# Weight splits placed behind the treatment of a result and bounded to four tiles ahead; the first input laid out by features

## The reference, cut to what matters

```
qkv = x @ w_qkv;  q, k, v = split(qkv, 3)
q = apply_rope(q) * 64 ** -0.5;  k = apply_rope(k)
for each block of 128 queries, each head, both maps m:
    p[m] = softmax(where(allowed, q[m] @ k[m].T, min))
    a = p[0] - lam * p[1];  o = a @ v
o = rms_norm(o) * (1 - lambda_init);  mix = o @ w_o
x = layer_norm(alpha * x + mix)
x = layer_norm(alpha * x + (silu(gate) * up) @ w_out)      # gate, up = split(x @ w_in, 2)
```

## Time and profile before

| | |
|---|---|
| timed runs | 1912.24 us median (1912.19 to 1922.69) |
| the profiled execution's own time | 1916.28 us |
| its span, first to last instruction | 1914.6 us |
| PE busy | 1841.1 us, 96% of the span |
| DVE, ACT, POOL busy | 903.6, 664.8, 57.9 us |
| mean granted TensorE clock | 0.984 of full speed |
| hi: 236 + 53 instructions, mean | 1059 and 1057 ns |
| lo: 236 + 53 instructions, mean | 1225 ns |

### The profile page before, as it was taken

One profiled execution on the slowest core, in us unless ns is written; L12 is line 12 of the kernel. 1 busy time (PEld: TensorE's weight loads), 2 busy tenths in 40 slices (PEclk: granted clock), 3 DMA queues, 4 the chain that ended last, 5 costly groups with the idle time before them and its releaser, 6 DMA issues.

```text
span 1914.6 us, 21555 instructions
## 1 busy us (share of the span) xinstructions
PE 1841.1 (96%) x8656; PEld 1480.3 (77%) x8656; DVE 903.6 (47%) x1544; ACT 664.8 (35%) x1084; POOL 57.9 (3%) x68
## 2 busy tenths in 40 slices
PE   8987879999999999999999999999999999999998
PEld 6755557888888897566698888888887788888886
DVE  3576766533333362555573333336544474334343
ACT  4233432422223232555432232222446444323231
POOL 0221110000000000000000000000000000000000
PEclk9989899999999999999999999999999999999999
DMA  7321111423333323222223333333321324333221
GB/s 235 98 77 49 66 53 56 132 77 112 98 99 99 120 87 107 66 67 67 83 89 99 93 95 99 99 98 96 100 73 60 110 67 122 99 100 99 77 78 44
DMA packets 217306, 174.51 MB, mean 91 GB/s; under 512 B 8899, under 2 KB 177765, under 8 KB 217206
## 3 DMA queue, kind: packets, MB, share of 16 engines
q1 hardware_dynamic: 217206, 173.13, 29.7%
HBM read 170.97 MB, written 7.38 MB: 93 GB/s over the span
## 4 chain that ended last, share of the span: by engine, by line
PE 90%; DVE 5%; ACT 3%; issue 2%; DMA 0%; SPq 0%; ACTq 0%
PE ps L526 27%; PE ps L527 27%; PE ps L528 27%; PE ps L823 2%; PE ps L783 2%; ACT whi L989 1%; PE ps L803 1%; PE ps L833 1%; PE ps L845 1%; PE ps L722 1%; DVE wlo L1263 1%; PE ps L793 0%; PE ps L934 0%; DVE arena L1289 0%; DVE arena L1285 0%
## 5 line engine op out<-in xcount | busy, mean ns | idle before, releaser
L1263 DVE TENSOR_TENSOR wlo<-raw,whi 128x1024 fp32r<-128x1024 f32 x236 | 288.3, 1225 | 588.8 <-ACT whi L989 586.6
L989 ACT ACTIVATE whi<-raw 128x1024 fp32r<-128x1024 f32 x236 | 248.8, 1059 | 578.3 <-PE ps L528 570.8
L526 PE MATMUL ps<-xh,whi 128*128 128x512 f32 (+1 forms) x1176 | 444.9, 378 | 0.0
L528 PE MATMUL ps<-xh,wlo 128*128 128x512 f32 (+1 forms) x1176 | 433.2, 368 | 0.0
L527 PE MATMUL ps<-xl,whi 128*128 128x512 f32 (+1 forms) x1176 | 433.1, 368 | 0.0
L526 PE MATMUL ps<-whi,hh 128*128 128x512 f32 x648 | 257.1, 397 | 7.2 <-DVE hl L1467 3.8
L526 PEld LDWEIGHTS ps<-xh,whi 128*128 128x128 f32 x1176 | 224.0, 190 | 39.0 <-issue 4.6
L528 PE MATMUL ps<-whi,hl 128*128 128x512 f32 x648 | 253.8, 392 | 0.0
L527 PE MATMUL ps<-wlo,hh 128*128 128x512 f32 x648 | 253.6, 391 | 0.0
L528 PEld LDWEIGHTS ps<-xh,wlo 128*128 128x128 f32 x1176 | 223.2, 190 | 37.4
L527 PEld LDWEIGHTS ps<-xl,whi 128*128 128x128 f32 x1176 | 223.6, 190 | 36.7 <-issue 2.9
(11 more groups left out here) (198 smaller groups left out, 2021.7 us busy)
## 6 DMA issues: line engine op xcount, KB each, us to landing
raw<-in_ffn_w_in SPq DMA_DIRECT2D x88, 512.0 KB, 3.9
raw<-in_w_ff SPq DMA_DIRECT2D x64, 512.0 KB, 4.0
raw<-in_ffn_w_out SPq DMA_DIRECT2D x44, 512.0 KB, 3.8
raw<-in_a_w_qkv SPq DMA_DIRECT2D x24, 512.0 KB, 5.2
raw<-in_w_in SPq DMA_DIRECT2D x20, 512.0 KB, 3.8
raw<-in_kv_w SPq DMA_DIRECT2D x16, 512.0 KB, 3.7
bias_skewed<-bias_rows SPq DMA_DIRECT2D x8, 640.0 KB
raw<-in_a_w_o SPq DMA_DIRECT2D x8, 512.0 KB, 4.7
```

The lines of the kernel that those rows point to most:

```text
L526: e.matmul(o, ah, bh, start=start, stop=False)
L528: return e.matmul(o, al, bh, start=False, stop=stop)
L989: e.activation(self.parts(m)[0], self.raw[:, m % RAW, :], ACT.Copy).then_inc(s.hi, 1)
L1263: e.tensor_tensor(lo, self.raw[:, m % RAW, :], f32(hi), ALU.subtract).then_inc(s.lo, 1)
```

## The change

A constant `AHEAD = 4` replaces the bound of eight. `pump` is no longer called by `done`; it is called by `take` as before, and once, for at most one split, at the end of `post`, behind the post step. The host hands the kernel a second copy of x, laid out by features; SP loads it in four pieces of 512 KB, each ahead of the weight tile that is used with it, and the transpositions and the split of their banks are gone for this first input. The x by positions, which the first residual needs, is loaded in the step `prepare_a`. The loads of norm vectors and tables come behind the first half of the value rows, and those rows now go one tile at a time. Of the two `xt` steps below, the first is ACT's and the second DVE's; the loop over `RAW` is SP's.

```
-        while most and self.slots and not self.waiting and self.n_split < len(self.tiles) + SPLIT + EXTRA:
+        while most and self.slots and not self.waiting and self.n_split < len(self.tiles) + AHEAD:
...
     def done(self, tile, sem, value):
...
-        self.pump()
...
     def post(self, job):
...
             self.step("post", job, None)
+        self.pump(1)
...
     def network(self):
         self.step("table", LN_EXP)
-        for t in range(4):
-            self.feat(0, t)
-            self.xsplit(0, t)
+        values = self.rows("v", ("a_w_qkv", 2048), 0, 8, hh=False)
+        for i in range(16):
+            if i % 4 == 0:
+                self.step("xt", i // 4)
+            next(values)
         self.step("load_norm", 1)
         self.step("load_a")
-        self.run(self.rows("v", ("a_w_qkv", 2048), 0, 8, grouped=True, hh=False))
+        self.run(values)
...
-                    w.wait_ge(s.xl, x_at + 2 * t + 2)
+                    w.wait_ge(s.xl, x_at + (8 if x_at else k0 + 2))
...
+            elif what == "xt":
+                j, = arg
+                w.wait_ge(s.xt[j], 16)
+                e.activation(self.xh[:, 2 * j:2 * j + 2, :], self.xt[:, 2 * j:2 * j + 2, :],
+                             ACT.Copy).then_inc(s.xh, 2)
...
+            elif what == "xt":
+                j, = arg
+                c = (slice(None), slice(2 * j, 2 * j + 2), slice(None))
+                w.wait_ge(s.xh, 2 * j + 2)
+                e.tensor_tensor(self.xl[c], self.xt[c], f32(self.xh[c]), ALU.subtract).then_inc(s.xl, 2)
...
                 if r.kind == "res":
                     w.wait_ge(s.rows, r.value)
+                    w.wait_ge(s.x[t], 16)
...
+        for m in range(RAW):
+            c = (slice(None), slice(2 * m, 2 * m + 2), slice(None))
+            e.dma_start(self.xt[c], ap["c_xt"][c]).then_inc(s.xt[m], 16)
+            weights(m)
         e.dma_start(self.ident[:], ap["c_ident"]).then_inc(s.ident, 16)
-        for t in range(4):
-            e.dma_start(self.x[:, t, :], ap["x"][0, t * 128:t * 128 + 128, :]).then_inc(s.x[t], 16)
-        for m in range(RAW):
-            weights(m)
...
             elif what == "prepare_a":
+                for t in range(4):
+                    e.dma_start(self.x[:, t, :], ap["x"][0, t * 128:t * 128 + 128, :]).then_inc(s.x[t], 16)
...
+def features_first(x):
+
+    return np.ascontiguousarray(x[0].reshape(S, 8, 128).transpose(2, 1, 0))
```

More of the change, by code:

```diff
@@ L24 @@
 EXTRA = 2
+AHEAD = 4
 FFN_GROUPS = [(0, 6), (6, 8), (14, 8)]
@@ L199, in projections, with rows @@
             self.run(self.quarters(*w))
-    def rows(self, kind, source, row0, nk, k_first=0, grouped=False, hh=True, norm=None, group=0):
+    def rows(self, kind, source, row0, nk, k_first=0, hh=True, norm=None, group=0):
         blocks = [(k_first + k) % nk for k in range(0, nk, 2)]
@@ L213, in rows @@
                 runs = [[k] for k in blocks[:-n]] + [blocks[-n:]]
-            elif grouped:
-                runs = [blocks[:n]] + [[k] for k in blocks[n:]]
             else:
@@ L535, in __init__ @@
         self.raw = [new(f"raw{i}") for i in range(RAW)]
-        self.x = [new(f"x{i}") for i in range(4)]
+        self.x, self.xt = [new(f"x{i}") for i in range(4)], [new(f"xt{i}") for i in range(4)]
         self.g = [new(f"g{i}") for i in range(3)]
@@ L631, in __init__ @@
         self.qk_a.append([ar(BASE + 13824 + i * 512, 512) for i in range(3)])
+        self.xt = ar(BASE + 8192, 4096).rearrange("p (k c) -> p k c", k=8)
         self.V = ar(BASE + 4096, 4096).rearrange("p (t c) -> p t c", t=4)
@@ L713, in tensor @@
                     w.wait_ge(*freed[b])
-                    if norm == 0:
-                        w.wait_ge(s.x[t], 16)
-                    elif norm < 4:
+                    if norm < 4:
                         w.wait_ge(s.ln, 8 * (norm - 1) + 2 * t + half + 1)
@@ L993, in scalar @@
                 for half, b in enumerate(banks):
-                    w.wait_ge(s.feat, 8 * norm + 2 * t + half + 1)
+                    w.wait_ge(s.feat, 8 * (norm - 1) + 2 * t + half + 1)
                     e.activation(self.xh[:, half * 4:half * 4 + 4, t * 128:t * 128 + 128],
@@ L1104, in scalar @@
                 if t >= 2:
-                    w.wait_ge(s.feat, 8 * norm + 2 * (t - 2) + 2)
+                    w.wait_ge(s.feat, 8 * (norm - 1) + 2 * (t - 2) + 2)
                 elif norm == 5:
-                    w.wait_ge(s.feat, 8 * 4 + 2 * (t + 2) + 2)
+                    w.wait_ge(s.feat, 8 * 3 + 2 * (t + 2) + 2)
                 e.activation(self.y[t % 2], self.x[:, t, :], ACT.Square,
@@ L1815 @@
     given["a_w_qkv"] = halves_first(given["a_w_qkv"])
+    given["c_xt"] = features_first(given["x"])
     given.update(constants())
```

## The result

The kernel after takes 1863.74 us (median of four runs, 1862.75 to 1865.22), the kernel before, run beside it, 1914.38 us. The ratio is 0.9728, 95% interval 0.9697 to 0.9760: faster by 2.7%. The profiled execution took 1865.22 us, with a span of 1863.5 us and a mean granted clock of 0.995, where the one before had 0.984. Its span is 51.1 us shorter.

A forecast was written before the change was run, and what follows sets the result against it. PE was taken to bound the full networks, with waits and lowered clock in the first attention. Gains of 29 there, 5.5 at the start and 1 in the second attention, 35.5 us, gave 1880.8, or 1877 us as median; range 1854 to 1902.

The forecast's parts named there:

- Ten waits by 2.32 us, 23 in all: First attention: PE's ten waits on the treatment (line 1289) each fall by hi and lo's 2.32 us, at most 23 us.
- 5 us given back, 2 us gained on line 1459: First attention: lo delaying softmax work costs 5 us (0 to 8.6); two softmax-result waits shorten by 2 us.
- The clock, 9 us: First attention: waits fall by 44%, so 44% of the 21 us lost by clock, 9 us, comes back.
- the clock coming back entirely: First attention, rival: remaining short waits no longer lower the clock, 12 us more return, 1865 us; chance 0.13.
- The start, 5.5 us: Kernel start: without the transpositions PE starts at 8.9 instead of 14.26 us; 5.5 us less, between 1.5 and 8.
- The second attention, 1 us (0 to 4): Second attention: the post step's ACT copy gets out from behind hi; 1 us less, between 0 and 4.
- SP, POOL and the networks, nothing: Moved loads on SP and POOL's queued addition are covered, and full PE hides the move in the networks; no change.
- POOL's port, nothing: DVE's lo beside POOL's work: no charge, since lo kept its duration beside a mask; blocking rival 1888 us, chance 0.05.
- DVE as the bound: First attention, rival: DVE becomes the bound because lo is only moved; 17 us gained with the start, 1896 us; chance 0.17.

The follow-up runs named there:

- experiment 4: Kernel after with the old bound of eight, so each split follows directly behind the treatment of the job that frees its slot; 1867.61 us, ratio 0.9723.
- experiment 5: Kernel after with each split one step earlier, ahead of the treatment, in a slot freed a job earlier; 1886.79 us, ratio 0.9832.
- experiment 11: Kernel after plus 40 small matmuls before the first product, just-treated bank passed over once, bound of eight in the first attention; 1866.15 us, ratio 0.9725.
- experiment 12: Kernel after plus 25 small matmuls before the first product, just-treated bank passed over once, bound of eight in the first attention; 1863.01 us, ratio 0.9726.
- experiment 1: Kernel after with splits placed as before (bound of eight, pump in `done`, none in `post`), only the start differing from the kernel before; 1926.13 us, ratio 1.0038.
- experiment 9: Kernel after with the bound of four only until the first half of the value rows, then bound of eight and pump in `done`; ratio 0.9986.

## Why the prediction was right, step by step

Direction, size and mechanism were right: 1877 us forecast, 1863.74 measured, inside 1854 to 1902. The terms against the traces, for 35.5 us forecast and 51.1 us of span found (the execution forecast from, at 1916.28 us, lay 4.0 us above the median then known; the profiled execution of the kernel after lies 1.5 above its own):

- **Ten waits by 2.32 us, 23 in all.** Measured 32.6 - 10.3 = 22.3. Experiments 4 and 5 show that the place of lo behind the treatment makes them, as the step had it. Its other half, that hi no longer waits for a running job, is true in the trace (ACT's waits for PE ahead of hi fall from 19.5 us in 12 to 2.8 in one) but adds nothing here once lo stands behind (experiment 4).
- **5 us given back, 2 us gained on line 1459.** The line costs 5.4 us in two waits before and 5.9 in seven after, so both came and all but cancelled. The two waits of 2.83 and 2.58 us are 1.26 and 1.30 now, 2.9 us less; five new ones of 0.4 to 1.0 us make 3.4. With each lo directly behind its treatment it is 6.3. PE's idle time fell by 23.1 us, not by 20: these two terms were 2.5 us too gloomy, the first 0.7 too hopeful, and a wait for ACT fell by 1.3.
- **The clock, 9 us.** In the first attention this is the step that was mis-sized most: 13 us came back by PE's busy time, 15 by the clock column. The proportion to the waiting time was the error. In the kernel before, each of the 12 spells of low clock in the stage starts within 1.3 us of the end of a wait of 1.9 us or more. Of such waits it has 14, and the kernel after four, with three spells: their number falls faster than the sum of the waits (45.5 to 22.4 us). Nine spells at 1.6 us (experiments 11 and 12) are 14 us. So of the named rivals, the clock coming back entirely (1865) lay nearest to the result. That its time fits is luck in part: 6 us of the 21 are still lost, and the second attention brought 5.5 us that it did not have. The Trainium skill, "TensorE: Matmul & The Clock Gate", section "HAM oscillation — how this bites in real kernels", has the cost of a fallen clock paid anew behind each wait for the next slice, so that it goes with the number of such waits. The traces agree that it goes by spells (1.6 us each); that of two equal waits (2.04 and 2.03 us) one has a spell and the other none, they show beyond it.
- **The start, 5.5 us.** Measured 6.0. PE started at 8.38 (8.9 forecast) and the fourth pair was not late. The first 13 products at 0.43 us cost 2.6 us, as the prediction let stand. But the term was reckoned as if it stood by itself; experiments 1 and 9 show that it needs the bound at the start, and that without it the first scores come 6.8 us later than before.
- **The second attention, 1 us (0 to 4).** Measured 6.5, outside the bounds given. The split out of ACT's way was the right place: the wait on line 1490 went from 4.9 to 0.5 us, and 3.2 us of the gain go where the bound of eight is back (experiment 4). One spell of low clock at its start went too. That PE loses only 7.7 us there bounded the idle time, not what could come back with the clock; and most of those 7.7 us were waits for the very copy that the step moved.
- **SP, POOL and the networks, nothing.** Right: 363.87 against 363.88 us in the network, and no wait up to 79 us in spite of the loads that moved.
- **POOL's port, nothing.** Nearly right in size, wrong in its reason. The earlier trace rows showed lo beside a mask. Behind the treatment lo meets POOL's rotary addition instead, and there the trace shows blocking (last section). POOL has time for its own part; but four times the longer addition holds up an operation of the softmax on DVE (line 1468) by 0.9 us, and PE's waits on line 1472 behind these four are 1.30, 0.43, 0.13 us and none, so an estimate is that at most 0.9 + 0.43 + 0.13 = 1.5 us are lost.
- **DVE as the bound.** It did not come: no wait of PE on DVE in the stage is longer than before, though DVE is busy for 159.98 of 197.15 us, 81%. (The prediction's 79% is 163 of 208 us, 78%.)
- **Not foreseen:** 1.6 us lost in the mixer, to one more spell of low clock while PE was full, and 3.6 gained in its last part, where a wait of 1.85 us became 0.28 and the spell behind it went. Why the clock falls with no wait ahead of it stays open.

The differences add up: 36.3 - 29 = 7.3 in the first attention (3.1 of it waits, 4.2 clock), 0.5 at the start, 5.5 in the second attention and 2 behind it, 15.3 of the 51.1 - 35.5 = 15.6 us.

## What to carry to other kernels

On an engine that takes its work in order, put what is needed last behind what somebody waits for now; look for preparation of later tiles ahead of the operation that frees a bank. A bound on how far preparation runs ahead is a way to place it, and an early start of another stage may need that bound as well. When waits shrink, count the spells of low clock behind them in the trace and price each spell that may go; here a share of the waiting time underrated it.

## What the runs showed of the hardware

**lo and POOL's addition block each other.** POOL's groups of costliest instructions in the kernel after (busy us, mean ns) have the addition at 1785 ns, where the kernel before had 1272:
```profile
L1616 POOL TENSOR_TENSOR arena<-arena 128x512 f32<-128x512 f32 x16 | 28.6, 1785 | 113.6 <-DVE arena L1301 113.4
```
In order of time, first POOL ahead of DVE, then DVE ahead of POOL:
```profile
97.55 1.26 POOL L1616 TENSOR_TENSOR arena<-arena 128x512 f32<-128x512 f32 x1 [0.28 <-DVE arena L1301]
97.59 2.30 DVE L1269 TENSOR_TENSOR wlo<-raw,whi 128x1024 fp32r<-128x1024 f32 x1 [0.20 <-ACT whi L989]
...
111.61 1.22 DVE L1269 TENSOR_TENSOR wlo<-raw,whi 128x1024 fp32r<-128x1024 f32 x1
111.84 2.14 POOL L1616 TENSOR_TENSOR arena<-arena 128x512 f32<-128x512 f32 x1 [13.03 <-DVE arena L1301]
...
112.94 1.06 DVE L1468 TENSOR_TENSOR stat<-stat,small 128x1 f32<-128x1 f32 x1
```
The one that starts second ends later by most of what was left of the first: lo takes 2.30 us and not 1.22, with 1.22 left of the addition, or the addition 2.14 and not 1.26, with 0.99 left of lo. From 79 to 276 us this hit lo once. Of the 16 additions the ten that start inside a lo take 1.94 to 2.14 us and the other six 1.26 to 1.27, 16 x 0.51 = 8.2 us dearer in all, which is the 8.0 us that POOL's busy time grew. The last line is the next step: an operation on one column, 0.16 us elsewhere, takes 1.06 and ends with the longer addition. This comes four times, and the softmax result stands behind it. The Trainium skill, "SBUF — State Buffer", section "Who interferes with whom", has this rule, and the prediction set it aside by the masks; for the addition of two inputs the trace agrees with it. For the masks the kernel before shows both: lo was not longer where it started behind one (83.77 us), but the one mask that started 0.5 us into a lo was, with 2.14 us and not 1.56:
```profile
106.23 2.14 POOL L1611 TENSOR_SCALAR arena<-arena,small 128x512 f32<-128x512 f32 x1
```

**The clock column can hide a slow start.** From 8.38 to 60 us it says 1.00 in the kernel after, although the first 13 products are 0.43 us apart and all later ones 0.23; read the spacing.

**The kernel before varies more than the kernel after,** 1911 to 1925 us over all its runs beside these experiments, against 1862.75 to 1865.22, and its time goes with the mean granted clock: 0.986 or 0.987 in every run under 1914 us, 0.978 to 0.980 in every run above 1919. The whole spread is 13.5 us, and 0.009 x 1914 = 17 us of clock is enough for it. What makes the clock fall oftener in one execution than in another is not shown.
